# Filler products beside HGRN2's later levels and its last part, with a new order of the lanes and a reworked unit norm, in a one-core decoder layer

## The chip, the core and the metric

The kernel runs on one core of a Trainium2 chip. The metric is the device time of one execution in microseconds (us). The core has TensorE (PE, matrix products; PEld is its weight load), VectorE (DVE), ScalarE (ACT), GpSimd (POOL) and SyncE (SP, which issues transfers). Each engine works through its own queue in order, and the queues meet only at semaphores.

## The reference, cut to what matters

One decoder layer for 512 prompt tokens and 8 samples of 4 tokens (T = 544 columns in all): four mixers in parallel (block-sparse attention, Mamba-2, HGRN2, gated DeltaNet), an output projection, cross-attention to 256 memory tokens, and a SwiGLU network. All in float32. The parts that the change touches:

```python
def gla_chunked(q, k, v, log_f, s0):          # HGRN2
    ...
        att = jnp.einsum('blhk,bshk,blshk->blsh', qc, kc, dec)
        o = (jnp.einsum('blsh,bshv->blhv', att, vc)
             + jnp.einsum('blhk,bhkv->blhv', qc * jnp.exp(bcum), S))
    ...
def l2_norm(x, eps=1e-6):
    return x * lax.rsqrt(jnp.sum(x * x, axis=-1, keepdims=True) + eps)
    ...
    # gated DeltaNet, gdn_mixer
    q = l2_norm(q.reshape(b, L, GDN_HEADS, GDN_DK)) * GDN_DK ** -0.5
    k = l2_norm(k.reshape(b, L, GDN_HEADS, GDN_DK))
    beta = jax.nn.sigmoid(beta_raw)
    ...
        kb = kc * bc[..., None]               # beta times k; v is taken times beta too
```

The samples' block-sparse attention (`moba_sample`) reads 2048 past keys and values for each sample from a paged cache, 16 pages of 128 tokens each.

## The kernel before, in words

The work is a row of stages, and every engine passes `stage_ended` between them: inputs, `win` (input projection), `ssm` (Mamba-2 and HGRN2, with three other things beside them), `gdn`, `wout`, cross-attention, `wxo` with the first half of the network, `wdn`. The change lies in the stage `ssm`, which goes from about 283 to 554 us.

**The lanes.** In that stage each engine has four generators, and the string `LANES` (L2882) says in which order their steps are issued. All engines follow the same string, so it fixes the order of each engine's queue:

- `m` is the main lane: `ssm_tensor`/`ssm_vector`/`ssm_scalar` (19 steps), then `hgrn_tensor`/`hgrn_vector`/`hgrn_scalar` (22 steps). Of HGRN2, steps 20 to 27 are the eight prompt levels (j = 0 to 7: 16 products of 64x128 by 128 each, into banks 0 to 3), steps 28 to 30 the three sample levels, step 31 the first turn of the last part (`tail_tensor`), and steps 32 to 41 its five token tiles, two steps each, called here 0a, 0b, 1a, ... 4b. Step 18 is the last step of Mamba-2 with products.
- `p` is the samples' attention (`moba_sample_*`, 111 steps): 66 key steps k0 to k65 (turn four pages' worth of keys on TensorE, copy them on ScalarE, score the earlier ones), four steps without work for TensorE in which VectorE ranks the blocks (L1501 to L1517) and ScalarE takes the exponentials (L1553), five steps pt0 to pt4 that turn the probabilities, and 32 value steps v0 to v31, each one quarter of pages (four loads of 128 KB). There are NPG = 4 page buffers; the load of quarter n + 4 waits until quarter n has been used (`ms_values_used`), and SP and POOL issue the quarters in turn (`load_pages`, L449).
- `u` is the unit norm of DeltaNet's q and k (`unit_*`, 17 steps), and the spreading of beta over k and v. TensorE sums squares to 4 rows through `headsel`, ScalarE makes the inverse root on 4 partitions, and TensorE spreads the 4 rows over 128 partitions through `pairsel`: 8 products of 272 columns for the sums and 12 for the six spreads. VectorE multiplies out of PSUM banks 5 and 6.
- `n` is Mamba-2's norm (`ssm_norm_*`, 3 steps), through bank 4.

Before, seen from the `m` steps, the keys run until step 19; the norm is in the segments behind steps 20 to 22; pt0 is behind step 21; v0 and v1 are behind level 4 (step 24); the values then go two to a segment and end behind 3b; the unit norm goes from level 4 to 1b; the product `vpick` (L1443 on, out of the attention's result) stands ahead of 4b.

**A prompt level.** For level j + 1 VectorE writes differences (two operations), ScalarE takes their exponential (L2377), VectorE multiplies q and k by it, and then VectorE merges level j from PSUM (L2309, four operations). TensorE's next level waits for the products of q and k and for a free bank of the four.

**The last part** (`tail_tensor`, run = 0 for HGRN2). Step ia turns tile i + 1; step ib does the state and output products of tile i and waits for copies by VectorE (`tail_tok_out`).

`mm` (L257) is the plain product in float32 (recorded as two instructions each), `tr` (L260) the transpose, `bank(b)` one of eight PSUM banks of 512 columns. `ident` and `lev` are constants in SBUF.

Of the kernel before, what the change touches and what calls it, by code (L numbers as in the profile page):

```python
# [19 lines left out]
ALU = mybir.AluOpType  # L20
# [47 lines left out]
def build(nc, a, o):  # L68
# [7 lines left out]
    def S(name):  # L76
        if name not in sems:
            sems[name] = ctx.enter_context(nc.semaphore(name))
        return sems[name]

    with ctx:
# [25 lines left out]
        def bank(i):  # L107
            return PS[i // 2][:, i % 2, :]
# [5 lines left out]
        def carve(buf, at, *shape):  # L114
            n = 1
            for s in shape:
                n *= s
            v = buf[:, at:at + n]
            if len(shape) == 2:
                v = v.rearrange("p (a b) -> p a b", b=shape[1])  # L120
            elif len(shape) == 3:
                v = v.rearrange("p (a b c) -> p a b c", b=shape[1], c=shape[2])
            return v
# [133 lines left out]
        def mm(out, lhsT, rhs, start, stop):  # L257
            return nc.tensor.matmul(out, lhsT, rhs, start=start, stop=stop, skip_group_check=True)  # L258

        def tr(out, in_, k):  # L260
            return nc.tensor.transpose(out, in_, ident[0:k, 0:k])  # L261

# [117 lines left out]
        g_A = carve(PROJ, base + 2176, 2176)  # L380
        g_N = carve(PROJ, base + 2 * 2176, 2176)
        g_QK = carve(PROJ, base + 3 * 2176, 2176)
        g_sq = carve(XN, 2 * DH, 2, T)
        g_kb = carve(XN, 2 * DH, 2, T)
        g_norm = XN[0:H, 1216:1216 + T], SC[0:H, 8528:8528 + T]

        m = Carver(XN, 4 * T)
        t_tok = m(512)
# [995 lines left out]
        def moba_sample_tensor(pe):  # L1384
# [57 lines left out]
                yield  # L1442
            yield  # L1443
            pe.wait_ge(S("satt_o"), 1)
            pe.wait_ge(S("g_beta"), 6)
            pick = ident.rearrange("p (g e h t) -> p g e h t", e=2, h=H, t=TS)
            for e in range(2):
                for c_ in range(2):
# [202 lines left out]
        def half(ap, j):  # L1651
            return ap[:, j * HT:(j + 1) * HT]

        def spread_norm(pe, n):

            hp, kind = n % 2, n // 2
            src = rows[:, 2, :] if kind == 2 else g_norm[kind]
            for j in range(2):
                last = mm(bank(5 + j)[:, 0:HT], pairsel[0:H, hp, :], half(src, j), True, True)
            last.then_inc(S("rows_spread"), 1)  # L1660

        def unit_tensor(pe):
            yield
            for x in range(2):
                pe.wait_ge(S("satt_pt_out"), 5)
                pe.wait_ge(S("g_sq"), x + 1)
                if x:
                    pe.wait_ge(S("g_root"), 1)
                for hp in range(2):
                    for j in range(2):  # L1670
                        last = mm(bank(5 + j)[0:H, 0:HT], headsel[:, hp, :], half(g_sq[:, hp, :], j), hp == 0, hp == 1)
                last.then_inc(S("g_sum"), 1)
                yield
                yield
            pe.wait_ge(S("g_root"), 3)
            for n in range(6):
                if n:
                    pe.wait_ge(S("g_beta"), n)
                spread_norm(pe, n)
                yield  # L1680
                yield

        def unit_scalar(s):
            def squares(x):
                if x:
                    s.wait_ge(S("g_sum"), x)
                for hp in range(2):
                    last = A.activation(g_sq[:, hp, :], (gq, gk)[x][:, hp, :], ACT.Square)
                last.then_inc(S("g_sq"), 1)

            squares(0)
            yield
            yield
            for x in range(2):
                s.wait_ge(S("g_sum"), x + 1)
                for j in range(2):
                    last = A.activation(half(g_norm[x], j), two(5)[j][0:H, :], ACT.Ln, bias=eps[0:H, :])
                last.then_inc(S("g_root"), 1)
                if x == 0:
                    squares(1)  # L1700
                    yield
                    yield
            s.wait_ge(S("g_root"), 2)
            for x in range(2):
                last = A.activation(g_norm[x], g_norm[x], ACT.Exp, scale=-0.5)
            last.then_inc(S("g_root"), 1)
            yield
            for _ in range(12):
                yield

        def unit_vector(v):
            for _ in range(5):
                yield
            for n in range(6):
                yield
                hp, kind = n % 2, n // 2
                v.wait_ge(S("rows_spread"), 2 + n + 1)
                for j in range(2):
                    if kind == 0:
                        last = V.scalar_tensor_tensor(half(gq[:, hp, :], j), half(gq[:, hp, :], j), SCALE, two(5)[j], ALU.mult, ALU.mult)  # L1720
                    elif kind == 1:
                        last = tt(half(gk[:, hp, :], j), half(gk[:, hp, :], j), two(5)[j], ALU.mult)
                    else:
                        v.wait_ge(S("g_beta"), 4)
                        tt(half(g_kb[:, hp, :], j), half(gk[:, hp, :], j), two(5)[j], ALU.mult)
                        last = tt(half(gv[:, hp, :], j), half(gv[:, hp, :], j), two(5)[j], ALU.mult)
                last.then_inc(S("g_beta"), 1)
                yield


# [330 lines left out]
        def tail_tensor(pe, run, att, kd, qe, vT, kbg, N):  # L2061
# [17 lines left out]
            for i, (t0, w, _) in enumerate(TILES):  # L2079
# [22 lines left out]
                    last.then_inc(S("tail_w"), 1)  # L2102
                if i + 1 < NT:
                    turn(i + 1)
                yield
                pe.wait_ge(S("tail_tok_out"), 5 * run + i + 1)
                if gdn:
# [19 lines left out]
                if sample:  # L2127
                    pe.wait_ge(S("tail_vm"), run + 1)
                    for h in range(H):
                        r = slice((h % 2) * 64, (h % 2) * 64 + 64)  # L2130
                        last = mm(bank(tail_s_st[run][h // 2])[r, :], t_tok[0:w, h * 64:(h + 1) * 64], vm_of(run)[0:w, h * 512:(h + 1) * 512], True, True)
                    last.then_inc(S("tail_st"), 1)
                yield

        t_rt = sm(2, NS)
# [199 lines left out]
        def hgrn_tensor(pe):  # L2335
# [3 lines left out]
            for (lo, hi), nt, w, nl in lv_groups():  # L2339
                for j in range(nl):  # L2340
# [14 lines left out]
                        m_ += 1  # L2355
                    if j:
                        n += 1
                    yield
            yield from tail_tensor(pe, 0, h_att_of, h_k1[:, 0], h_q1[:, 0], proj[:, C_HI:C_HI + 2, :], None, None)

# [95 lines left out]
        def gdn_scalar(s):  # L2456
            hgrn_norm_scalar(s, 0)
            for i, (t0, w, _) in enumerate(TILES):
                s.wait_ge(S("g_m"), i + 1)
                ex = hl(g_p1[:, i % 4, :], w)  # L2460
                A.activation(ex, ex, ACT.Exp).then_inc(S("g_exp"), 1)
                if i < 4:
                    s.wait_ge(S("rows_spread"), 8 + i + 1)
                    A.activation(half(g_logd[:, i // 2, :], i % 2), bank(3 + 4 * (i % 2))[:, 0:HT], ACT.Copy).then_inc(S("rows_spread_out"), 1)
            s.wait_ge(S("rows_spread_out"), 4)
            link(A.activation(g_kbg, g_logd, ACT.Exp), "s")
# [408 lines left out]
        def mixer_lane(eng, ssm, hgrn):  # L2875
# [3 lines left out]
            yield from hgrn  # L2879


        LANES = "m".join(["pp"] + ["pppp", "ppp"] * 9 + ["ppp"] + ["ppn"] * 3 + ["pp"] + ["ppu"] * 7 + ["ppuu"] * 5  # L2882
                         + ["pp"] * 5 + ["p"])

        def lanes(main, pages_, unit, norm):
            steps = {"m": main, "p": pages_, "u": unit, "n": norm}
# [148 lines left out]
```

## Time and profile before

| | us |
|---|---|
| median of 3 runs | 1513.37 |
| lowest, highest | 1507.18, 1522.45 |
| the profiled execution, device time | 1517.02 |
| its span, first to last instruction | 1515.3 |
| TensorE busy in the span | 1358.2 (90%) |
| VectorE, ScalarE, GpSimd busy | 658.7, 467.9, 442.6 |
| mean granted TensorE clock | 0.907 of 2.4 GHz |

A granted clock of 1.00 is 2.4 GHz and 0.50 is 1.2 GHz; a value between them is a stretch in which both occur. Times of rows are us from the span's start. TensorE's matmul ends are modelled, so two neighbouring groups may overlap by some tenths of a microsecond.

### The profile page before, as it was taken

What the parts mean: (1) busy time and instruction counts of PE and PEld (TensorE: products, weight loads), DVE (VectorE), ACT (ScalarE), POOL (GpSimd) and SP (SyncE); (2) the same over time, 40 slices, a digit from 0 to 9 for tenths busy, and PEclk for the clock granted to TensorE, in tenths of its full rate; (3) what the DMA queues carried; (4) which work ended last, traced back from release to release, by engine and by line L of the source; (5) the groups of instructions that cost most, each with busy time, mean ns of one, the idle gap of its engine ahead of it and who ended that gap; (6) DMA issues with size and microseconds to landing.
All of it is one profiled execution on the core that took longest, in us unless ns stands there. A gap on an engine that the chain in (4) does not pass through costs nothing.

```text
span 1515.3 us, 24848 instructions
## 1 busy us (share of the span) xinstructions
PE 1358.2 (90%) x10080; PEld 1184.4 (78%) x10080; DVE 658.7 (43%) x1104; ACT 467.9 (31%) x769; POOL 442.6 (29%) x370
## 2 busy tenths in 40 slices
PE   5997999889767976888989898989899999989999
PEld 4997987656554556787879784439899999989998
DVE  4569944254665236653242924310763333330003
ACT  3322244254233014123345423203532222222221
POOL 5424431323103402003525050003234433434330
PEclk8998999879757556998969999999999999999999
DMA  4222230346306630003333040451223223222321
GB/s 122 79 62 70 74 114 1 118 147 192 106 0 196 183 111 1 1 7 119 112 113 98 29 167 22 169 185 56 70 76 93 84 86 96 84 77 77 91 64 60
DMA packets 177556, 136.85 MB, mean 90 GB/s; under 512 B 15011, under 2 KB 165972, under 8 KB 177442
## 3 DMA queue, kind: packets, MB, share of 16 engines
q1 hardware_dynamic: 167906, 113.85, 24.8%
q0 software_dynamic: 7200, 20.23, 4.4%
q8 instruction: 80, 1.31, 0.4%
q10 hardware_dynamic: 2336, 1.18, 0.3%
q14 instruction: 34, 0.28, 0.1%
HBM read 127.27 MB, written 7.96 MB: 89 GB/s over the span
## 4 chain that ended last, share of the span: by engine, by line
PE 75%; DVE 15%; ACT 4%; issue 2%; DMA 2%; POOL 1%; SPq 1%; DVEq 0%; POOLq 0%; ACTq 0%
PE PS L258 69%; PE PS L261 6%; DVE PROJ L1746 2%; DVE SC L626 1%; DVE PROJ L626 1%; DVE XN L887 1%; DVE XT L626 1%; DVE XN L626 1%; POOL W_LO L242 1%; DMA W_scratch<-in_cache_moba_v 1%; DVE PROJ L1747 1%; DVE XN_parts L878 1%; DVE RSQ L885 0%; DVE OM L1595 0%; DMA PROJ<-in_x_sample 0%
## 5 line engine op out<-in xcount | busy, mean ns | idle before, releaser
L242 POOL TENSOR_TENSOR W_LO<-W,W_HI 128x1024 fp32r<-128x1024 f32 (+1 forms) x130 | 317.3, 2445 | 797.8 <-ACT W_HI L233 797.8
L258 PE MATMUL PS<-XN_parts,W_HI 128*128 128x272 f32 x1184 | 341.9, 289 | 0.0
L258 PE MATMUL PS<-OM_parts,W_HI 128*128 128x272 f32 x960 | 279.0, 291 | 0.0
L258 PE MATMUL PS<-SC_parts,W_HI 128*128 128x272 f32 (+2 forms) x832 | 246.7, 296 | 14.7 <-POOL W_LO L242 13.5
L258 PE MATMUL PS<-SC_parts,W_LO 128*128 128x272 f32 (+2 forms) x832 | 243.1, 292 | 0.0
L258 PEld LDWEIGHTS PS<-XN_parts,W_HI 128*128 128x128 f32 x1184 | 224.6, 190 | 0.0
L258 PE MATMUL PS<-OM_parts,W_LO 128*128 128x272 f32 x704 | 203.9, 290 | 0.0
L233 ACT ACTIVATE W_HI<-W 128x1024 fp32r<-128x1024 f32 (+1 forms) x130 | 134.1, 1041 | 207.5 <-PE PS L258 207.5
L258 PEld LDWEIGHTS PS<-OM_parts,W_HI 128*128 128x128 f32 x960 | 183.2, 191 | 0.1
L258 PEld LDWEIGHTS PS<-SC_parts,W_HI 128*128 128x128 f32 x832 | 159.3, 191 | 19.3 <-POOL W_LO L242 12.5
L258 PEld LDWEIGHTS PS<-SC_parts,W_LO 128*128 128x128 f32 x832 | 159.1, 191 | 0.0
L258 PE MATMUL PS<-PROJ_parts,W_HI 128*128 128x272 f32 (+2 forms) x608 | 153.1, 294 | 5.0 <-DVEq L2873 5.0
L258 PEld LDWEIGHTS PS<-OM_parts,W_LO 128*128 128x128 f32 x704 | 132.3, 188 | 0.0
L258 PEld LDWEIGHTS PS<-PROJ_parts,W_HI 128*128 128x128 f32 x608 | 109.1, 193 | 5.4 <-DVEq L2873 5.3
L258 PE MATMUL PS<-PROJ_parts,W_LO 128*128 128x272 f32 (+2 forms) x256 | 75.7, 296 | 0.0
L258 PE MATMUL PS<-SC,XN 64*64 64x4 f32 (+3 forms) x384 | 69.6, 327 | 0.0
L449 POOL DMA_DIRECT2D W_scratch<-in_cache_moba_v x64 | 34.3, 536 | 113.8 <-PE PS L258 83.4
L626 DVE TENSOR_TENSOR SC<-SC 128x272 f32<-128x272 f32 (+6 forms) x68 | 36.8, 544 | 70.5 <-ACT SC L820 50.9
L1147 ACT ACTIVATE PROJ<-PS 128x512 f32<-128x512 f32 (+1 forms) x76 | 44.9, 597 | 65.1 <-PE PS L261 52.8
L261 PE MATMUL PS<-CN,W_scratch 128*128 128x128 f32 x272 | 51.4, 319 | 14.1 <-ACT SC L1554 12.2
L258 PE MATMUL PS<-SC 64*128 64x128 f32 (+7 forms) x404 | 52.7, 345 | 11.7 <-DVE PROJ L626 5.2
L258 PE MATMUL PS<-PROJ,XN 128*128 128x128 f32 (+3 forms) x280 | 43.3, 306 | 20.1 <-DVE XN L626 19.6
(375 smaller groups left out, 2259.6 us busy)
## 6 DMA issues: line engine op xcount, KB each, us to landing
W<-in_w_gu SPq DMA_DIRECT2D x44, 512.0 KB, 3.7
W<-in_w_in SPq DMA_DIRECT2D x30, 512.0 KB, 3.6
W_scratch<-in_cache_moba_k SPq DMA_DIRECT2D x64, 128.0 KB, 2.7
W_scratch<-in_cache_moba_k POOLq DMA_DIRECT2D x64, 128.0 KB, 2.6
W_scratch<-in_cache_moba_v SPq DMA_DIRECT2D x64, 128.0 KB, 2.1
W_scratch<-in_cache_moba_v POOLq DMA_DIRECT2D x64, 128.0 KB, 2.8
W<-in_w_xkv SPq DMA_DIRECT2D x16, 512.0 KB, 3.5
W<-in_w_down SPq DMA_DIRECT2D x16, 512.0 KB, 3.6
```

The costliest lines, as they stand in the source:

```text
L233: nc.scalar.activation(hi_lo(n)[0], raw_chunk(n), ACT.Copy)\
L242: nc.gpsimd.tensor_tensor(hi_lo(n)[1], raw_chunk(n), hi_lo(n)[0].bitcast(F32), ALU.subtract).then_inc(S("weights_split"), 1)
L258: return nc.tensor.matmul(out, lhsT, rhs, start=start, stop=stop, skip_group_check=True)
L261: return nc.tensor.transpose(out, in_, ident[0:k, 0:k])
L449: eng.dma_start(pages[:, n % NPG, i, :], cache[0].rearrange("g p h d -> g p (h d)")[bass.ds(ids[i], 1)].rearrange("g p n -> (g p) n"))\
L626: return V.tensor_tensor(out, x, y, op)
L878: V.scalar_tensor_tensor(lo(k)[:, TOKENS[run][j]], XT[:, k, TOKENS[run][j]], par(GAINS[run][1] + k), hi(k)[:, TOKENS[run][j]].bitcast(F32) ...
L887: last = V.scalar_tensor_tensor(xn[:, k, c_], xn[:, k, c_], par(GAINS[run][0] + k), rsq[:, c_], ALU.mult, ALU.mult)
L1147: return A.activation(o_, i_, ACT.Copy)
L1746: V.scalar_tensor_tensor(dst[:, d:SEQ], src[:, 0:SEQ - d], wt[3 - d], dst[:, d:SEQ], ALU.mult, ALU.add)
L1747: last = V.scalar_tensor_tensor(ds_, win_[:, :, 3 - d:7 - d], wt[3 - d], ds_, ALU.mult, ALU.add)
```

## The change

1. `warm(b, n)` is new: n products of the constant `ident` (128x128) with 512 columns of the constant `lev`, into bank b, which nobody reads. It is called in `hgrn_tensor` behind the products of prompt level 4 (8 products) and of levels 5, 6 and 7 (2 each), into bank 4; and in `tail_tensor` for run 0 in steps 0a to 3a and 0b to 2b (2 each), into bank 2. That makes 28 products.
2. `LANES` is rewritten. Now the key steps go four to a segment and end behind step 17; the step with the blocks' ranking and the exponentials is still behind level 1; the norm is behind steps 20 to 22; pt0 and pt1 are behind level 3, pt2 and pt3 behind level 4, pt4 and v0 behind level 5, then values two to a segment; v29, v30 and v31 are behind 4a, and `vpick` behind 4b. The unit norm's nine steps start behind the last sample level and end behind 3a.
3. The unit norm works on full rows: ScalarE squares one 128x544 tile (`g_sqs`, three buffers), TensorE sums it with the block matrix `blk64` (two products of 272 columns, result on all 128 partitions), ScalarE takes Ln and Exp, VectorE multiplies once from SBUF. Four such units, then two spreads of beta as before: 12 products in place of 20.

```diff
@@ build @@
+        def warm(b, n):
+            for _ in range(n):
+                mm(bank(b), ident, lev[:, 0:4, :].rearrange("p a b -> p (a b)"), True, True)
...
-        g_sq = carve(XN, 2 * DH, 2, T)
+        g_sqs = [carve(XN, 2 * DH + i * T, T) for i in range(3)]
...
@@ moba_sample_tensor @@
             pe.wait_ge(S("satt_o"), 1)
-            pe.wait_ge(S("g_beta"), 6)
+            pe.wait_ge(S("g_beta"), UNITS + 2)
@@ unit_tensor @@
+        UNITS = 4
+        UNIT_STEPS = 9
...
         def unit_tensor(pe):
+            for x in range(UNIT_STEPS):
+                n = x - 1
+                if 0 <= n < UNITS:
+                    if n == 0:
+                        pe.wait_ge(S("satt_pt_out"), 5)
+                    else:
+                        pe.wait_ge(S("g_root"), 2 * n - 1)
+                    pe.wait_ge(S("g_sq"), n + 1)
                     for j in range(2):
+                        last = mm(bank(5 + j)[:, 0:HT], blk64, half(g_sqs[n % 3], j), True, True)
+                    last.then_inc(S("g_sum"), 1)
+                elif x in (5, 7):
+                    if x == 5:
+                        pe.wait_ge(S("g_root"), 2 * UNITS - 1)
+                    else:
+                        pe.wait_ge(S("g_beta"), UNITS + 1)
+                    for j in range(2):
+                        last = mm(bank(5 + j)[:, 0:HT], pairsel[0:H, x // 7, :], half(rows[:, 2, :], j), True, True)
+                    last.then_inc(S("rows_spread"), 1)
                 yield
+        def unit_scalar(s):
+            for x in range(UNIT_STEPS):
+                n = x - 2
+                if 0 <= n < UNITS:
+                    s.wait_ge(S("g_sum"), n + 1)
+                    for j in range(2):
+                        last = A.activation(half(g_sqs[n % 3], j), two(5)[j], ACT.Ln, bias=eps)
+                    last.then_inc(S("g_root"), 1)
+                    s.wait_ge(S("g_root"), 2 * n + 1)
+                    A.activation(g_sqs[n % 3], g_sqs[n % 3], ACT.Exp, scale=-0.5).then_inc(S("g_root"), 1)
+                if x < UNITS:
+                    if x == 3:
+                        s.wait_ge(S("g_beta"), 1)
+                    A.activation(g_sqs[x % 3], unit_of(x), ACT.Square).then_inc(S("g_sq"), 1)
                 yield
         def unit_vector(v):
+            for x in range(UNIT_STEPS):
+                n = x - 2
+                if 0 <= n < UNITS:
+                    v.wait_ge(S("g_root"), 2 * n + 2)
+                    V.scalar_tensor_tensor(unit_of(n), unit_of(n), SCALE if n < 2 else 1.0, g_sqs[n % 3], ALU.mult, ALU.mult)\
+                        .then_inc(S("g_beta"), 1)
+                elif x in (6, 8):
...
@@ tail_tensor @@
                 if i + 1 < NT:
                     turn(i + 1)
+                if run == 0 and i < 4:
+                    warm(2, 2)
                 yield
...
                     last.then_inc(S("tail_st"), 1)
+                if run == 0 and i < 3:
+                    warm(2, 2)
                 yield
@@ hgrn_tensor @@
                     if j:
                         n += 1
+                    if w == P and j >= 4:
+                        warm(4, 8 if j == 4 else 2)
                     yield
@@ lanes @@
-        LANES = "m".join(["pp"] + ["pppp", "ppp"] * 9 + ["ppp"] + ["ppn"] * 3 + ["pp"] + ["ppu"] * 7 + ["ppuu"] * 5
-                         + ["pp"] * 5 + ["p"])
+        LANES = "m".join(["pp"] + ["pppp"] * 14 + ["ppp"] * 3 + ["p", "p", "pn", "pn", "n", "pp", "pp", "pp"] + ["pp"] * 4
+                         + ["ppu"] * 9 + ["pp", "pppp", "pp"])
```

## Rows read from the trace of the kernel before

**Rows 1.** Page, part 2: busy tenths and TensorE's granted clock, 40 slices.
```profile
PE   5997999889767976888989898989899999989999
...
PEclk8998999879757556998969999999999999999999
```
**Rows 2.** Page, part 4: the chain that ended last, by engine.
```profile
PE 75%; DVE 15%; ACT 4%; issue 2%; DMA 2%; POOL 1%; SPq 1%; DVEq 0%; POOLq 0%; ACTq 0%
```
**Rows 3.** Windows, TensorE: stretch, length, busy (instructions), granted clock, DMA share, GB/s.
```profile
444.00:455.00 11.00, 8.88 (x52) 0.50 0.01 1
460.00:473.00 13.00, 12.94 (x152) 1.00 0.53 172
473.00:477.00 4.00, 0.51 (x16) 0.91 0.73 240
489.00:506.00 17.00, 16.85 (x92) 0.50 0.60 180
506.00:523.00 17.00, 17.00 (x95) 0.50 0.51 148
523.00:532.00 9.00, 8.68 (x75) 0.94 0.71 201
538.00:551.00 13.00, 12.85 (x94) 0.50 0.00 0
551.00:585.00 34.00, 25.76 (x136) 0.50 0.29 93
```
**Rows 4.** Timeline, TensorE, 392 to 447 us: start, length; idle before in brackets.
```profile
392.36 3.69 PE L258 MATMUL PS<-PROJ,SC 32*128 32x512 f32 x8
395.99 0.43 PE L258 MATMUL PS<-PROJ,W 128*32 128x128 f32 x8
...
399.57 0.43 PE L258 MATMUL PS<-PROJ,W 128*32 128x128 f32 x8 [0.33 <-ACT PROJ L1147]
...
409.44 5.10 PE L258 MATMUL PS<-SC 64*128 64x128 f32 x32 [5.15 <-DVE PROJ L626]
426.69 1.12 PE L261 MATMUL PS<-CN,W_scratch 128*128 128x128 f32 x4 [12.15 <-ACT SC L1554]
427.60 2.02 PE L258 MATMUL PS<-SC,CN 128*128 128x272 f32 x4
429.55 5.13 PE L258 MATMUL PS<-SC 64*128 64x128 f32 x32
...
446.12 5.10 PE L258 MATMUL PS<-SC 64*128 64x128 f32 x32 [3.22 <-DVE PROJ L2309]
```
**Rows 5.** Timeline, VectorE, 411 to 440 us.
```profile
411.00 0.74 DVE L1501 SCALAR_TENSOR_TENSOR W_scratch<-XN,SM,W_scratch 128x512 f32<-128x512 f32 x1
...
436.42 3.53 DVE L1972 RECIPROCAL RSQ<-RSQ 128x544 f32<-128x544 f32 x1
```
**Rows 6.** Timeline, ScalarE, 431 to 433 us.
```profile
431.55 1.06 ACT L2377 ACTIVATE W<-W 128x1024 f32<-128x1024 f32 x1
```
**Rows 7.** Timeline, TensorE, 453 to 537 us.
```profile
453.15 1.94 PE L258 MATMUL PS<-W_scratch,PROJ 128*32 128x256 f32 x16
...
471.80 0.32 PE L258 MATMUL PS<-PROJ,W 64*32 64x32 f32 x8
...
477.12 1.93 PE L258 MATMUL PS<-W_scratch,PROJ 128*32 128x256 f32 x16 [3.61 <-DMA W_scratch<-in_cache_moba_v]
...
489.15 0.69 PE L261 MATMUL PS<-CN,SC 128*128 128x128 f32 x2 [5.66 <-DVE SC L626]
...
492.06 2.18 PE L258 MATMUL PS<-XN,CN 4*128 4x272 f32 x4
...
509.66 0.70 PE L258 MATMUL PS<-XN 128*64 128x64 f32 x8
...
515.02 1.93 PE L258 MATMUL PS<-W_scratch,PROJ 128*32 128x256 f32 x16
...
535.16 1.08 PE L258 MATMUL PS<-W_scratch,PROJ 128*32 128x256 f32 x8 [1.15 <-DMA W_scratch<-in_cache_moba_v]
```

More of the change, by code:

```diff
@@ L382, in build @@
         g_QK = carve(PROJ, base + 3 * 2176, 2176)
-        g_sq = carve(XN, 2 * DH, 2, T)
+        g_sqs = [carve(XN, 2 * DH + i * T, T) for i in range(3)]
         g_kb = carve(XN, 2 * DH, 2, T)
-        g_norm = XN[0:H, 1216:1216 + T], SC[0:H, 8528:8528 + T]
         m = Carver(XN, 4 * T)
@@ L1652, in half @@
             return ap[:, j * HT:(j + 1) * HT]
[L1654 to L1660, printed above, removed]
-        def unit_tensor(pe):
[L1663 to L1669, printed above, removed]
-                    for j in range(2):
[L1671 to L1680, printed above, removed]
+        UNITS = 4
@@ new lines, in build, with unit_of @@
+        UNIT_STEPS = 9
+        def unit_of(n):
+            return (gq, gk)[n // 2][:, n % 2, :]
+        def unit_tensor(pe):
+            for x in range(UNIT_STEPS):
[6 more added lines that the diff above has]
+                    pe.wait_ge(S("g_sq"), n + 1)
+                    for j in range(2):
+                        last = mm(bank(5 + j)[:, 0:HT], blk64, half(g_sqs[n % 3], j), True, True)
[8 more added lines that the diff above has]
+                    last.then_inc(S("rows_spread"), 1)
@@ L1681, in unit_tensor @@
                 yield
         def unit_scalar(s):
[L1684 to L1708, printed above, removed]
+            for x in range(UNIT_STEPS):
[11 more added lines that the diff above has]
+                    A.activation(g_sqs[x % 3], unit_of(x), ACT.Square).then_inc(S("g_sq"), 1)
@@ L1709, in unit_scalar @@
                 yield
         def unit_vector(v):
[L1712 to L1724, printed above, removed]
+            for x in range(UNIT_STEPS):
[5 more added lines that the diff above has]
+                elif x in (6, 8):
+                    hp = x // 8
+                    v.wait_ge(S("rows_spread"), 2 + hp + 1)
+                    v.wait_ge(S("g_beta"), UNITS)
+                    for j in range(2):
@@ L1725, in unit_vector @@
                         tt(half(g_kb[:, hp, :], j), half(gk[:, hp, :], j), two(5)[j], ALU.mult)
                         last = tt(half(gv[:, hp, :], j), half(gv[:, hp, :], j), two(5)[j], ALU.mult)
-                last.then_inc(S("g_beta"), 1)
+                    last.then_inc(S("g_beta"), 1)
                 yield
@@ L2462, in gdn_scalar @@
                 if i < 4:
-                    s.wait_ge(S("rows_spread"), 8 + i + 1)
+                    s.wait_ge(S("rows_spread"), 4 + i + 1)
                     A.activation(half(g_logd[:, i // 2, :], i % 2), bank(3 + 4 * (i % 2))[:, 0:HT], ACT.Copy).then_inc(S("rows_spread_out"), 1)
```

## The prediction, made before the changed kernel was run

> **What bounds the kernel now.** I began with the page's busy slices. TensorE is at 8 or 9 tenths for most of the span, but of slices 10 to 15 (379 to 606 us) five are at 6 or 7, and it is there that the granted clock falls to 5 to 7 tenths [rows 1]. The chain that ended last is 75% TensorE and 15% VectorE [rows 2]. So a microsecond of TensorE work taken from that stretch counts, and one added counts too, unless TensorE stands waiting there anyway. The windows then give the clock by stretch [rows 3]: 0.50 at 444 to 455 (early levels), 1.00 at 460 to 473 (levels 6 and 7), falling after the idle stretch 473 to 477, then 0.50 through 489 to 523 although TensorE is busy in 33.85 of those 34 us, 0.94 at 523 to 532, and 0.50 again for the samples' tile (538 to 551) and the first part of the next stage (551 to 585). The timeline shows what ends each wait: VectorE (5.15 us ahead of level 1, 3.22 ahead of level 4, 5.66 ahead of the last part's first turn), the softmax's exponentials (12.15 us ahead of pt0), and transfers of value pages (3.61 us, 1.15 us) [rows 4, 7]. The stretch is therefore three things by turns: a chain through VectorE and ScalarE up to level 4, TensorE at one clock or the other in the later levels and the last part, and transfers where a quarter's buffer came free late.
>
> A change of this kernel has to be over about 1%, 15 us, to be told from none.
>
> **Prices.** Four products of 512 columns took 3.69 us at full clock, 0.92 each [rows 4]; two of 272 columns took 2.02 us at half clock [rows 4], and half of that at full is taken as 1.0. By columns one filler product at half clock is 1.85 to 1.9 us. The filler loads 128 weight rows where the 3.69 us row loads 32; bounds 0.85 and 1.0 us at full clock, and I take 0.92. The 28 products cost 26 us at full clock and 52 at half.
>
> **Keys four to a segment.** Before, k61 to k65 come after Mamba-2's last products (the 3.69 us row at 392.36) and fill 395.99 to 400.0, while VectorE already runs the chain that ends in level 1 at 409.44 [rows 4]. In the new string these five steps stand ahead of those products. TensorE's sum is the same, but the chain starts 4.0 us later with nothing beside it. L1501 (0.74 us, behind level 0's merge before [rows 5]) now stands ahead of level 1's differences. Level 1 is thus 4.7 us late, at 414.1. Bounds: 0, if waits in the key steps hide it, to 6.
>
> **Levels 2 and 3 ahead of pt0.** The 12.15 us wait for the exponentials goes from TensorE's queue: level 2 (5.13 us) now runs in it [rows 4]. But level 3 needs the exponential at 431.55 [rows 6], which on ScalarE stands behind the softmax's. That comes 4 us later with everything, and about 1.9 earlier because pt0's copy (0.6) and the wait for it (1.2) no longer stand in front: 433.6. Level 3 then starts at about 436.7, where it stood before; but VectorE's reciprocal of 3.53 us, at 436.42 before [rows 5], starts at about 438.7, and the differences of level 4 come after it. Level 4 starts 2.2 us later: 446.1 becomes 448.3 [rows 4]. What leaves TensorE's wait is late next on VectorE. Bounds -3 and +6.
>
> **Level 4 to the sample levels.** Before, v0 is used at 453.15 and the first sample level is at 471.80 [rows 7]. After: level 4 5.1 us at half clock, to 453.4; eight fillers. Before the clock rose some 13 us after level 4 began; with dense products I let it rise some 9 us after, so two fillers at 1.85 and six at 0.92 make 9.2, and with a third nearer half 9.7: to 463.1. Then pt2 and pt3 1.2, level 5 2.8 (half the 5.1), two fillers 1.85, pt4 and the own block 1.6: v0 at 470.5, 17 us later than before. Then v0, level 6, fillers, two values, level 7, fillers, two values: 0.5 + 2.8 + 1.85 + 1.1 + 2.8 + 1.85 + 1.1 = 12.0, plus 0.7 of small waits: first sample level at 483.2, 11.4 late. Two fillers a level hide in part behind VectorE (some 6 us a level), the eight do not. Bounds: 7.4 us for the eight if the clock rises at once, 14.8 if not before they end.
>
> **Sample levels to the first turn.** Before 471.8 to 489.15, 17.35 us: values with the 3.61 us wait [rows 7], two spreads, then VectorE's and ScalarE's preparation. From 477.12 on, two values, a spread and the level (1.9 + 2.2 + 0.4) end at 481.6, and the turn comes 7.5 later, 0.7 of it a norm product of VectorE that moves away. After: v3 and v4 are used at about 482.5; a quarter's reload took about 7 us where two were used together (v6 and v7 just ahead of 471.8, v10 at 477.1, less the time before the issue), so v7 and v8 are there at 490, the last sample level at 491.2, the turn 6.8 later: 498, 8.9 late. The waits for pages replace the spreads.
>
> **The last part.** Before: 489.15 to 536.2 (the end of v31) = 47.0 us [rows 7]. After, at half clock: a first half-step is two turns 1.3, two fillers 3.7, two values 1.94, a unit sum 2.0, together 8.9; at full 4.7. A second half-step with state is 5.4 at half (509.66 to 515.02 [rows 7]) and 3.0 at full, with fillers, values and sum 7.0 at full. TensorE stands still from about 492 to 498, so it starts at half clock; I let it be full from the middle of 0a: turn segment 5.3, 0a 7.5, 0b 4.4, 1a 4.7, 1b 7.0, 2a 3.7, 2b 7.0, 3a 3.7, 3b 4.1 = 47.4, to 545.4. The 14 fillers here (13 to 15 us) use up what full clock and the smaller unit norm give. Then v29, v30, v31 stand together behind 4a; v31's buffer is freed by v27, used at about 544.5, and its load takes about 7 us (v27's release to v31 took some 8 before, which is the 1.15 us wait at 535.16 [rows 7]): v31 ends at 552.5, 16.3 late.
>
> The unit norm loses 8 of 20 products. The nearest price for a spread is 2.18 us at half clock [rows 7]; 8 products are 8.7 us at half, 4 at full, and this is inside the sums above. On ScalarE a unit is two table loads, two halves of Ln, an Exp and a Square, which I estimate at under 5 us, in a stretch where ScalarE has no other work; VectorE loses operations. I cost it at nothing beyond that; if VectorE waits for an exponential, up to 1 us a unit.
>
> **The end.** Before, `vpick` and the wait ahead of it (2.4 us) came between v31 and the samples' tile; now they follow. 16.3 - 2.4 = +13.9. Nothing behind the stage is edited, and TensorE has another idle stretch there, so its clock at 551 to 585 is left at 0.50.
>
> **Sum.** 4.7, then 2.2, 11.4, 8.9, 16.3 and 13.9 are the lateness at each point, not terms to be added; the stage ends 13.9 us later: 1517.0 + 13.9 = 1531 against the profiled execution. That one is 3.7 us over the median of 1513.4, so the forecast in the terms of the median is 1527 us, 0.9% more. Its own range by the bounds above is 1514 to 1540.
>
> A rule against the trace. TensorE was busy in 33.85 of 34 us at 489 to 523 and its clock stayed at 0.50 [rows 3]. The Trainium skill (TensorE: Matmul & The Clock Gate, section Why this matters for your kernels) says to keep TensorE busy without gaps and it reaches the full clock. By that rule the last part would need no fillers, only unbroken work; this trace does not agree.
>
> **Rivals.**
> *The clock stays up (not slower).* The fillers raise the clock in the first of the eight (-2.3), it outlives the 6 us wait ahead of the last part (-5), the samples' tile runs at full clock (12 us become 7, -5), and so does the start of the next stage, where 25.8 busy us at half [rows 3] would fall by about 8 with VectorE's chain next in line. 13.9 - 20.3 = -6.4: 1510.6 against the profiled execution, 1507 in the median's terms. It decides itself at the idle stretch ahead of the turn: if the granted clock is still 1.00 in the first turn, this one holds. For it: the clock did hold from 523 to 532 with like work. Against: it fell after 473 to 477. [...]
> *The order of the lanes costs less than counted (same).* The key steps' waits hide the 4.7 us, and the page reloads keep ahead: the values lose only the fillers' time, about +3: 1520, or 1516 in the median's terms. For it: TensorE waits at few of the key steps, and SP and POOL are idle beside. Against: the wait of 3.61 us on a transfer.
> *The fillers don't lift the clock in the last part (slower).* Then 14 fillers cost 26 us, and the segments sum to 5.3 + 8.9 + 9.4 + 8.9 + 13.1 + 6.9 + 13.1 + 6.9 + 7.3 = 79.8 in place of 47.4; with v31 no longer waiting, some 28 us more: 1559, or 1555. For it: the busy stretch at 0.50. Against: the fillers use all rows and columns, where the work before had 4, 32 or 64.
>
> **How the numbers follow.** Forecast 0.42, clock stays up 0.25, order cheap 0.20, no lift 0.13. Faster by over 1%: 0.16 of the second and 0.04 of the third, 0.20. Slower by over 1%: 0.19 of the first (it stands just under the bound), 0.02 of the third, 0.13: 0.34. Within 1%: 0.46. The range reaches from 1500 (the clock stays up, with a little more from the smaller norm) to 1552; that leaves out the worse half of the last rival and the best end of the second.
>
> **What would show it.** Right: in the changed kernel's timeline level 1 starts at about 414, level 4 at 448, v0 at 470 or later, the first turn at 498, TensorE's clock 1.00 from about 510 to 545, and a wait on a value transfer ahead of v31. Wrong: v0 before 462; the clock at 1.00 in the samples' tile or at 555; or half clock between 510 and 540.

## The result, and the profile after

The changed kernel takes 1523.5 us (median of 20 runs, 1515.06 to 1531.08), the one before 1514.01 us (20 runs, 1507.18 to 1522.45). The ratio is 1.0059 with a 95% interval of 1.0043 to 1.0076: 9 us slower. The forecast was 1527. The profiled execution of the changed kernel took 1521.28 us with a span of 1519.7, that is 2.2 under its median, and the one of before was 3.0 over its own, so the spans of the two profiles lie only 4.4 us apart (1519.7 and 1515.3) where the medians lie 9.5 apart.

TensorE's timeline of the changed kernel, with the lines that answer to [rows 4, 7] (start, length, form, idle before it):

```profile
391.73 7.19 PE L258 MATMUL PS<-PROJ,SC 32*128 32x512 f32 x8
...
413.08 4.60 PE L258 MATMUL PS<-SC 64*128 64x128 f32 x32 [4.21 <-DVE PROJ L631]
...
421.03 5.10 PE L258 MATMUL PS<-SC 64*128 64x128 f32 x32 [2.24 <-DVE PROJ L2305]
435.90 5.10 PE L258 MATMUL PS<-SC 64*128 64x128 f32 x32 [9.76 <-DVE PROJ L2305]
...
447.16 4.62 PE L258 MATMUL PS<-SC 64*128 64x128 f32 x32 [5.13 <-DVE PROJ L2305]
451.71 7.13 PE L258 MATMUL PS<-CN 128*128 128x512 f32 x16
...
465.90 0.64 PE L258 MATMUL PS<-W_scratch,PROJ 128*32 128x256 f32 x8
...
477.80 0.32 PE L258 MATMUL PS<-PROJ,W 64*32 64x32 f32 x8
...
483.51 1.93 PE L258 MATMUL PS<-W_scratch,PROJ 128*32 128x256 f32 x16 [4.14 <-DMA W_scratch<-in_cache_moba_v]
...
488.01 1.94 PE L258 MATMUL PS<-W_scratch,PROJ 128*32 128x256 f32 x16 [2.20 <-DMA W_scratch<-in_cache_moba_v]
492.80 0.69 PE L266 MATMUL PS<-CN,SC 128*128 128x128 f32 x2 [2.86 <-DVE SC L631]
...
542.17 2.79 PE L258 MATMUL PS<-W_scratch,PROJ 128*32 128x256 f32 x24 [5.34 <-DMA W_scratch<-in_cache_moba_v]
...
561.71 3.97 PE L258 MATMUL PS<-SC,CN 128*128 128x272 f32 x8 [3.61 <-DVE SC L631]
```

In order: Mamba-2's last products (now at half clock, 7.19 us), levels 1, 2, 3 and 4, the eight fillers (7.13 us, all at full clock), v0, the first sample level, two waits for value pages, the first turn of the last part, v29 to v31, and the first products of the next stage. (The helper's transposes are L266 here, L261 before.)

The windows that answer to [rows 3] (stretch, length, busy, granted clock, DMA share, GB/s):

```profile
451.00:459.00 8.00, 8.00 (x27) 0.99 0.00 0
459.00:477.00 18.00, 17.64 (x148) 1.00 0.27 82
477.00:493.00 16.00, 6.80 (x89) 0.65 0.66 210
493.00:498.50 5.50, 5.50 (x28) 0.50 0.78 238
498.50:536.50 38.00, 38.00 (x278) 0.99 0.64 198
545.00:557.00 12.00, 12.00 (x80) 0.50 0.00 1
562.00:587.00 25.00, 24.89 (x129) 0.50 0.36 123
```

With the fillers in place the clock is 1.00 in the later levels and 0.99 over 38 us of the last part, where before it was 0.50 at 489 to 523; whether it is the fillers that raise it, run a1 below decides. The samples' tile and the next stage's start stay at 0.50. And the last part did not end earlier: from the turn (492.80) to the end of v31 (544.96) are 52.2 us, 47.0 before, with 5.34 us of waiting for pages ahead of v29. Counted from level 1, the turn comes at the same place in both kernels (79.7 us), v31 ends 5.1 us later, and the next stage follows v31 2.4 us sooner, since `vpick` has moved.

### The profile page after: what moved, and what is told of

Its sections match the earlier page's. It is cut to its first block, busy times and chain, and to the rows that moved or that the text cites. A ratio compares the mean times of both kernels' runs of the same rounds, so it can differ in the third digit from the quotient of the medians.

```text
span 1519.7 us, 24935 instructions
## 1 busy us (share of the span) xinstructions
PE 1358.7 (89%) x10120; PEld 1180.8 (78%) x10120; DVE 658.5 (43%) x1100; ACT 476.3 (31%) x779; POOL 442.7 (29%) x370
## 4 chain that ended last, share of the span: by engine, by line
PE 55%; DVE 7%; ACT 2%; issue 2%; POOL 1%; DMA 1%; POOLq 0%; DVEq 0%; ACTq 0%
PE PS L258 53%; PE PS L266 2%; DVE PROJ L631 1%; DVE XT L631 1%; DVE XN L892 1%; DVE SC L631 1%; DVE XN L631 1%; DVE XN_parts L883 1%; DVE RSQ L890 0%; POOL W_LO L242 0%; DMA W_scratch<-in_cache_moba_v 0%; POOL PROJ_parts L242 0%; POOLq L444 0%; DVE OM L2687 0%; ACT W_HI L233 0%
## 5 line engine op out<-in xcount | busy, mean ns | idle before, releaser
L258 PE MATMUL PS<-SC 64*128 64x128 f32 (+7 forms) x404 | 50.4, 331 | 24.7 <-DVE PROJ L2305 17.1
L258 PEld LDWEIGHTS PS<-SC 64*128 64x128 f32 (+5 forms) x404 | 41.2, 215 | 34.0 <-DVE SC L631 23.1
L258 PE MATMUL PS<-SC,XN 64*64 64x4 f32 (+3 forms) x384 | 66.4, 318 | 0.0
L258 PE MATMUL PS<-OM_parts,PROJ_parts 128*128 128x272 f32 x256 | 55.2, 307 | 2.9 <-DVE XN_parts L883 1.6
```

## The experiments

The stretch up to Mamba-2's last products starts some microseconds earlier or later from execution to execution (389 to 398 us over these runs), so traces are compared from level 1 of HGRN2 to the first products of the next stage. This table has both readings for every run; the ratios are to the kernel before, timed beside it (its median was 1514.01 to 1515.93 us in the four rounds). Medians are of 20 executions for the first two rows, of 6 for d1, and of 9 to 12 for the others.

| run | level 1 to next stage, us | median, us | ratio (95%) |
|---|---|---|---|
| before | 146.0 | 1514.01 | |
| changed | 148.6 | 1523.50 | 1.0059 (1.0043 to 1.0076) |
| a1, no fillers | 139.3 | 1517.66 | 1.0016 (0.9994 to 1.0038) |
| a2, fillers in the levels only | 145.9 | 1520.21 | 1.0035 (1.0017 to 1.0054) |
| a3, fillers in the last part only | 142.4 | 1517.34 | 1.0021 (0.9994 to 1.0048) |
| a4, before plus fillers | 151.2 | 1522.72 | 1.0051 (1.0028 to 1.0073) |
| b1, before plus new unit norm | 145.2 | 1518.73 | 1.0023 (1.0005 to 1.0042) |
| b3, changed, values earlier | 149.5 | 1521.54 | 1.0039 (1.0014 to 1.0064) |
| c1, no fillers, keys as before | 139.1 | 1513.40 | 0.9994 (0.9972 to 1.0015) |
| c2, c1 with the reciprocal late | 132.7 | 1508.82 | 0.9964 (0.9942 to 0.9985) |
| d1, c2 with pt0, pt1 earlier | 130.4 | 1502.41 | 0.9922 (0.9892 to 0.9952) |
| d2, c2 with fillers in a wait | 134.4 | 1508.91 | 0.9962 (0.9940 to 0.9983) |
| d3, a1 with half value loads | 138.4 | 1515.58 | 0.9999 (0.9978 to 1.0019) |
| d4, changed with half value loads | 146.3 | 1524.16 | 1.0056 (1.0035 to 1.0077) |

The two columns do not say the same everywhere. The stretch is read from one execution of each kernel. That of c1 is 6.9 us shorter than before and its median is the same; that of c2 is 13.3 us shorter and its median some 5.5 us. What stands behind the stretch took between 955.9 and 964.3 us in these traces, where no edit touches it. The runs do not show where the difference goes, so a claim about the whole time rests on the ratio, and the stretch tells only where in the stage time was won or lost.

**a1 to a4: the fillers by themselves.** The theory after the result: the fillers buy the full clock in the last part and are worth about what they cost. The rival: they only cost.

```diff
 a1, a2:            (tail_tensor)
-                if run == 0 and i < 4:
-                    warm(2, 2)
...
-                if run == 0 and i < 3:
-                    warm(2, 2)
 a1, a3:            (hgrn_tensor)
-                    if w == P and j >= 4:
-                        warm(4, 8 if j == 4 else 2)
```

a4 puts the same lines into the kernel before. Expected:

> The changed kernel without its 28 filler products; new lanes and new unit norm stay. Theory (the fillers buy the full clock in the last part and are worth about what they cost): the last part runs at half clock for most of its length, v31 ends at 544 to 549 us (changed kernel: 544.9), and the time is within 4 us of the changed kernel's 1523.5. Rival (the fillers only cost): 26 us of products at full clock fall away and nothing slows, 1498.

> Only the 14 fillers behind levels 4 to 7. Theory: the turn ahead of the last part stays at 492 to 493, the last part runs at 0.50 for most of its length and takes 50 us or more in place of 43.5, time 1526 to 1531. Rival (the clock raised in the levels carries through, or needs no fillers): the last part takes 43.5 - 13 = 30 us or is held by page loads at 40, 1512 to 1518.

> Only the 14 fillers of the last part. Theory: v0 comes 5 to 7 us earlier than 465.9, the turn at 488 to 490, the last part at full clock as in the changed kernel, time 1518 to 1521. Rival (the eight fillers are free because VectorE or the page loads set the pace there): turn at 492 to 493 and 1522 to 1525.

> The kernel before with the 28 fillers at the same places; its own lanes and unit norm. Theory: the later levels lose some 6 us, the last part runs at full clock but with 14 fillers and takes as long as before (47 us), v31 at 541 to 543, time 1519 to 1521. Rival (the whole loss of the change is in the lanes, fillers neutral or better): 1508 to 1514.

Without fillers the changed kernel is 5.8 us faster (1523.50 against 1517.66), and its stretch 9.3 us shorter. Neither theory holds as it stood: not a draw, and not 26 us either. The two halves add up: from a1, the level fillers alone add 6.6 us to the stretch (a2) and those of the last part 3.1 (a3), together 9.7 against 9.3 measured. By the medians a2 adds 2.6 and a3 nothing, which is less than the 5.8 of both together; the intervals are too wide to say more. In a2 the turn stayed where it was counted from level 1 (80.3 us, 79.7 in the changed kernel), as expected, but the last part took 48.8 us and neither time forecast held. In a3 v0 came 7.2 us earlier counted from level 1 and the median lies just under the 1518 to 1521 expected. In the order of before (a4) the fillers cost 5.2 us of the stretch, ratio 1.0051, near the 1519 to 1521 expected. There they did shorten the last part, from 47.1 to 42.9 us, but the way from level 1 to it grew by 7.4 us and what follows v31 by 2.0.

The premise itself fell. This is TensorE of a1, with no filler anywhere:

```profile
471.06 0.32 PE L258 MATMUL PS<-PROJ,W 64*32 64x32 f32 x8
...
486.83 0.69 PE L266 MATMUL PS<-CN,SC 128*128 128x128 f32 x2 [2.76 <-DVE SC L631]
...
496.32 1.45 PE L258 MATMUL PS<-W_scratch,PROJ 128*32 128x256 f32 x16 [1.89 <-DMA W_scratch<-in_cache_moba_v]
...
521.34 1.93 PE L258 MATMUL PS<-W_scratch,PROJ 128*32 128x256 f32 x16 [3.70 <-DMA W_scratch<-in_cache_moba_v]
...
532.37 1.94 PE L258 MATMUL PS<-W_scratch,PROJ 128*32 128x256 f32 x16 [4.53 <-DMA W_scratch<-in_cache_moba_v]
535.89 1.08 PE L258 MATMUL PS<-W_scratch,PROJ 128*32 128x256 f32 x8 [1.59 <-DMA W_scratch<-in_cache_moba_v]
...
553.73 3.96 PE L258 MATMUL PS<-SC,CN 128*128 128x272 f32 x8 [3.61 <-DVE SC L631]
```

and its windows (stretch, length, busy, granted clock, DMA share, GB/s):

```profile
491.00:497.00 6.00, 4.11 (x53) 0.99 0.81 245
497.00:500.00 3.00, 3.00 (x14) 0.50 0.69 220
500.00:515.00 15.00, 12.86 (x116) 0.99 0.78 242
515.00:532.00 17.00, 9.14 (x80) 0.77 0.66 191
```

The last part starts at 486.83 and the clock is at 0.99 in 491 to 497 and 500 to 515 without any filler. What it meets then are pages: six waits in the last part, 13.9 us in all (2.8 before). v31 ends at about 537, 50 us after the turn; TensorE was busy for little more than half of 515 to 532. In a2 the clock was 1.00 at 510 to 525, again without fillers in that part. So most of the full clock was to be had without fillers once the order and the unit norm were new, and it was worth little, because a faster TensorE runs into the page loads. What the fillers cost is less than their own time because part of them stands where TensorE would have waited: from 456 to 546 us it waits 11.7 us for value pages in the changed kernel and 20.0 in a1.

**b1: is it the unit norm that lifts the clock?** The kernel before with the new `unit_*` functions only:

```diff
-        LANES = ... + ["ppu"] * 7 + ["ppuu"] * 5 + ["pp"] * 5 + ["p"]
+        LANES = ... + ["ppu"] * 9 + ["pp"] * 8 + ["p"]
```

> The kernel before with the new unit norm only: its own lanes, the nine unit steps one to a segment from level 4 to the last part's first turn, no fillers. Theory (the unit sums through the block matrix fill all rows and columns, and that, not the fillers, is what holds the clock up in the last part): granted clock over 0.85 from 495 to 525 where it was 0.50, stage end 5 to 8 us earlier counted from level 1, time 1508 to 1511. Rival (it only saves eight products): the last part stays at 0.50, time 1511 to 1515.

In between: the granted clock is 0.75 at 495 to 510 and 0.70 at 510 to 525 (0.50 and 0.53 before), the stretch only 0.8 us shorter, and the ratio 1.0023. The time forecast missed: I had 1508 to 1511. TensorE's waits for pages after the turn grew from 2.8 to 9.7 us here as well, and two waits on ScalarE's squares' chain (2.27 and 1.84 us) came in before it, since here the unit steps stand beside the levels, where ScalarE and VectorE are busy. The last part itself took 42.3 us in place of 47.1, but its first turn came 2.7 us later counted from level 1. That the sums over all rows and columns are what raises the clock is thus likely, not shown: b1 changes ScalarE's and VectorE's part with the sums and has gaps that the kernel before does not have, and no run changes the sums alone.

**b3: the three values behind 4a.**

```diff
-         + ["ppu"] * 9 + ["pp", "pppp", "pp"]
+         + ["ppu"] * 3 + ["pppu", "ppu", "pppu"] + ["ppu"] * 3 + ["pp", "pp", "pp"]
```

> The changed kernel with two value steps moved forward: three behind 0b and 1b, one behind 4a (before three behind 4a). Theory (v31's load waits for v27 alone): the 5.3 us wait ahead of v29 falls to about 1, time 3 to 4 us under the changed kernel, 1519 to 1521. Rival (the transfers are at their rate and the wait only moves): sum of page waits in the last part unchanged, 1522 to 1525.

Neither held in full. From 456 to 546 us TensorE waited 10.8 us for pages in six places, in the changed kernel 11.7 us in three; from the first turn on it is 4.1 us in three places against 5.3 in one:

```profile
486.19 1.94 PE L258 MATMUL PS<-W_scratch,PROJ 128*32 128x256 f32 x16 [4.65 <-DMA W_scratch<-in_cache_moba_v]
```

This wait of b3, its longest, stands ahead of the turn and answers to the 4.14 us at 483.51 in the changed kernel. The last part took 49.9 us (52.2), but the turn came 3.1 us later counted from level 1, and that was lost ahead of the edit for the most part: v0 was already 2.5 us later, in a place where the two kernels are the same. 1521.54 against 1523.50 is inside the uncertainty, so whether moving the values is worth 2 us isn't shown.

**c1 and c2: the order of the keys, and VectorE's reciprocal.**

```diff
 c1 (on a1): key segments as before, segment 20 "ppn"
 c2 (on c1): third step of the norm lane
-  ... "ppn", "pn", "n", ... "ppu", "pp", "pppp", "pp"
+  ... "ppn", "pn", "",  ... "ppu", "ppn", "pppp", "pp"
```

> The changed kernel without fillers, and with the key steps in the order of the kernel before (four and three in turn, Mamba-2's last products ahead of k61). Theory (the keys' packing delays the chain to level 1 by 4.7 us): level 1 starts 13.5 us after the end of Mamba-2's last products again but with five key steps beside it, and the time is 3 to 6 us under the run without fillers, 1511 to 1514. Rival (the packing costs nothing): equal to the run without fillers, 1516 to 1518.

> As the one before, and the norm's last step on VectorE (reciprocal and two products, 5 us) moves from behind level 2 to behind 3b. Theory (VectorE's chain sets levels 3 to 4): level 4 starts 5 us earlier counted from level 1 (29 in place of 34), the stage ends 3 to 5 us earlier, time 1506 to 1511. Rival (the values' page loads take it all back): level 4 earlier, but v31 within 1 us, time unchanged.

c1 is 4.3 us under a1, as expected, and the stretch behind level 1 is the same (139.1 and 139.3): what the keys' packing costs comes before level 1. The intervals of c1 and a1 overlap, so the size is uncertain. From the start of Mamba-2's last products to level 1 are 17.7 us in c1, 17.1 before, and 21.4 in a1 and in the changed kernel, where those products run at half clock (7.19 us in place of 3.69). In b3, with the same order of keys, they happened to run near full clock (3.93 us) and the distance was 18.1; so most of the longer distance is the clock. The forecast's reason, that five key steps of 4.0 us stand ahead of these products and no longer beside VectorE's chain, can't be read from the traces, because the start of these products moves by more than that from one execution to another; both costs together would be over 4.3 us. c2 shows VectorE's chain: level 4 starts 30.5 us behind level 1 (34.9 in c1, 34.1 in the changed kernel, 36.7 before), the stretch is 6.4 us shorter than c1's, and the kernel is faster than the one before, 0.9964. The time came as the theory said, and the stretch gained more than its 3 to 5 us. The theory's rival, in which the page loads take it all back, did not come:

```profile
409.33 5.10 PE L258 MATMUL PS<-SC 64*128 64x128 f32 x32 [5.15 <-DVE PROJ L631]
...
432.94 5.10 PE L258 MATMUL PS<-SC 64*128 64x128 f32 x32 [9.76 <-DVE PROJ L2301]
...
439.87 5.13 PE L258 MATMUL PS<-SC 64*128 64x128 f32 x32
...
476.50 0.69 PE L266 MATMUL PS<-CN,SC 128*128 128x128 f32 x2 [2.65 <-DVE SC L631]
```

**d1 and d2: what else stands in that wait.** TensorE still waits 9.76 us ahead of level 3 there (432.94 above is its start). d1 puts pt0 and pt1 into it; d2 puts fillers into it.

```diff
 d1 (on c2)
-  ... "ppn", "pn", "", ... "ppn", "pppp", "pp"
+  ... "ppn", "pn", "pp", ... "ppn", "pp", "pp"
 d2 (on c2, hgrn_tensor, behind level 2)
+                    if w == P and j == 2:
+                        warm(6, 5)
```

> As the run with the late reciprocal, and pt0, pt1 stand behind level 2 (in TensorE's 9.8 us wait), everything after them two steps earlier, so that 4a has v31 alone. Theory (the last part is paced by the reload of page buffers, so its end follows v0): v0 4 to 6 us earlier counted from level 1, v31 and the stage's end 4 to 7 us earlier, time 1502 to 1506. Rival (TensorE sets the pace): end moves by under 2 us, 1507 to 1510.

> As the run with the late reciprocal, and five fillers (bank 6) behind level 2, in the 9.8 us in which TensorE waits for VectorE. Theory (fillers cost nothing in a wait and raise the clock for levels 3 to 5): level 3 starts within 0.5 us of before, levels 3 and 4 take 2.8 us in place of 5.1, v0 3 to 5 us earlier, time 1505 to 1508. Rival (the clock stays at 0.50 and five fillers of 1.85 us end late, or VectorE sets levels 3 to 5): v0 unchanged within 1 us, 1508 to 1511.

TensorE of d1 (level 1, pt0 with pt1, the samples' own block ahead of v0, the turn, v31, the samples' tile, the next stage):

```profile
408.74 5.10 PE L258 MATMUL PS<-SC 64*128 64x128 f32 x32 [5.15 <-DVE PROJ L631]
...
426.00 1.97 PE L266 MATMUL PS<-CN,W_scratch 128*128 128x128 f32 x8 [3.42 <-ACT SC L1559]
...
443.57 1.13 PE L258 MATMUL PS<-W 32*128 32x256 f32 x4 [0.36 <-ACT W L1152]
...
475.92 0.69 PE L266 MATMUL PS<-CN,SC 128*128 128x128 f32 x2 [3.14 <-DVE SC L631]
...
519.19 0.64 PE L258 MATMUL PS<-W_scratch,PROJ 128*32 128x256 f32 x8 [1.76 <-DMA W_scratch<-in_cache_moba_v]
522.65 0.30 PE L258 MATMUL PS<-PROJ,XN 32*64 32x32 f32 x2 [2.82 <-DVE XN L2154]
...
539.12 3.97 PE L258 MATMUL PS<-SC,CN 128*128 128x272 f32 x8 [3.61 <-DVE SC L631]
```

The own block, and v0 behind it, come 34.8 us after level 1 in place of 41.8 in c2 (451.14 - 409.33), and the stage ends 2.3 us earlier. The median is 1502.41, ratio 0.9922 (0.9892 to 0.9952): this version beats both kernels, 11.6 us under the one before and 21 under the changed one (six executions), and has no filler. v0 moved by 7.0 us, the first turn by nothing (67.2 us behind level 1 in both; its wait is ended by VectorE), the end of v31 by 4.9 and the stage's end by 2.3. So the earlier values did not bring the turn forward, v31 came as early as the theory said, and half of that was lost again in 2.82 us of waiting for VectorE ahead of the samples' tile, which c2 does not have. The theory's 4 to 7 us at the stage's end did not come, though the time did (6.4 us by the medians, more than the trace of one execution explains).

d2 is the fair test of a filler that costs nothing:

```profile
423.44 5.39 PE L258 MATMUL PS<-CN 128*128 128x512 f32 x10
433.27 5.10 PE L258 MATMUL PS<-SC 64*128 64x128 f32 x32 [4.44 <-DVE PROJ L2301]
```

The five products took 5.39 us, at full clock for most of it, and level 3 started as late as in c2 (23.6 us behind level 1 both times). But 4.44 us of idle followed, and level 3 ran its 5.10 us at half clock all the same. v0 came 1.7 us earlier than in c2 and the next stage 1.7 later, and the time equals c2's (1508.91 and 1508.82), inside the rival's range. The theory was right that the fillers fit into the wait, and wrong about what follows. Here a raised clock that wasn't followed by work at once was lost.

**d3 and d4: bytes or issue?** Each value quarter is loaded by half its columns, so half of the sample attention's values is left out of both kernels.

```diff
+                w_ = 2 * P if n < 32 else P
-                    eng.dma_start(pages[:, n % NPG, i, :],
+                    eng.dma_start(pages[:, n % NPG, i, 0:w_],
```

> The changed kernel without fillers, and the value pages loaded by half their columns (the other half of each buffer keeps what was there; half of the attention's values is left out). Theory (page transfers set the pace of the last part once its clock is high): waits on value transfers in the last part fall from 13.9 us to under 4, the stage ends 7 to 10 us earlier, time 1507 to 1511. Rival (the waits are latency, not bytes): 1515 to 1519.

> The changed kernel with all its fillers and the same half loads (the same half of the values left out). Theory: the 4.1 and 2.2 us waits ahead of the last sample levels and the 5.3 us ahead of v29 shrink, time 1514 to 1518, and the fillers now cost more against the run without them (8 to 12 us, 6.5 with full loads), because less of them stands in page waits. Rival (fillers earn their clock): the two runs with half loads within 3 us.

Of d3 the rival won. With half the bytes the stretch shortens by 0.9 us (d3 against a1) and 2.3 (d4 against the changed kernel), and the times stay: 1515.58 and 1517.66, 1524.16 and 1523.50. From 456 to 546 us TensorE waited 19.7 us for value pages in d3 and 20.0 in a1. In d4 these waits fell from 11.7 to 9.9 us only, and its time forecast, 1514 to 1518, failed; that the fillers would cost 8 to 12 us with half loads came right (8.6 by the medians). GpSimd's timeline tells why. d3, then a1:

```profile
486.49 2.29 POOL L455 DMA_DIRECT2D W_scratch<-in_cache_moba_v  x4 [2.26 <-issue]
491.04 2.29 POOL L455 DMA_DIRECT2D W_scratch<-in_cache_moba_v  x4 [2.26 <-issue]
...
500.46 2.29 POOL L455 DMA_DIRECT2D W_scratch<-in_cache_moba_v  x4 [2.27 <-issue]
```

```profile
504.69 2.29 POOL L454 DMA_DIRECT2D W_scratch<-in_cache_moba_v  x4 [2.26 <-issue]
509.25 2.29 POOL L454 DMA_DIRECT2D W_scratch<-in_cache_moba_v  x4 [2.26 <-issue]
514.01 0.55 POOL L454 DMA_DIRECT2D W_scratch<-in_cache_moba_v  x1 [2.47 <-issue]
517.31 1.72 POOL L454 DMA_DIRECT2D W_scratch<-in_cache_moba_v  x3 [2.75 <-issue]
...
526.13 2.29 POOL L454 DMA_DIRECT2D W_scratch<-in_cache_moba_v  x4 [2.26 <-issue]
```

A quarter is four transfers of 2.29 us together, behind 2.26 us without a recorded operation; in the chain of waits these hold the reads of the four page numbers (L444, 0.29 us each recorded) and the gaps between them. That makes one quarter every 4.55 us from this queue, with 64 KB transfers as with 128 KB ones. GpSimd issues every second quarter, so two value steps cannot take less than 4.55 us for long, whatever TensorE's clock. In a1 the queue runs so without a rest from 472 to 533 us, all quarters from v7 to v31. The one exception is v25's, whose four transfers took 5.02 us because of a pause of 2.75 us behind the first (514.01 and 517.31 above); every trace of this case has it, its cause isn't shown, and behind it stands a1's 3.70 us wait. No run gave GpSimd fewer quarters to issue, so the issue rate is read from the timelines and not tested by an edit; what the edits rule out is the bytes.

In the changed kernel three quarters between 500 and 520 us wait for TensorE to free their buffer (their issues start at 501.87, 506.72 and 518.14, each 0.68 us behind the last use of the buffer). Behind them it is the queue that holds. The same queue ahead of v31:

```profile
531.06 1.70 POOL L454 DMA_DIRECT2D W_scratch<-in_cache_moba_v  x3 [0.33 <-issue]
535.02 2.29 POOL L454 DMA_DIRECT2D W_scratch<-in_cache_moba_v  x4 [2.26 <-issue]
539.57 2.29 POOL L454 DMA_DIRECT2D W_scratch<-in_cache_moba_v  x4 [2.25 <-issue]
```

The starts 535.02 and 539.57 are again 4.55 apart; they are v29's quarter and v31's. v31's buffer was free at 536.40, when v27 had been used, but the queue came to it 3.2 us later, 2.5 us more than those 0.68; it landed at 543.68, just ahead of its use at 543.85. The 5.34 us wait itself is for v29. Its buffer was free at 532.28, its issue began 2.7 us later, and its last transfer landed at 542.04, 5.3 us after that transfer was issued, where the median from 500 to 546 us is 2.7. SP issued a load of 512 KB in between, at 535.62; whether that is what delayed v29 isn't shown.

## Why the prediction was right, point by point

- **Direction and time.** Forecast 1527, 0.9% more; measured 1523.5, 0.6% more. That the path to the end of v31 gets longer was right, and its size was too large. That the fillers are partly paid back by the clock was not: a1 has most of that clock without them, and what made them cheap is that some stand in page waits. The last part's 54.5 us, forecast from a clock that the fillers buy, is therefore near the measured 52.2 in part by luck.
- **Keys four to a segment.** Forecast level 1 4.7 us late (414.1). It starts at 413.08, 3.6 late in one trace, and by c1 against a1 the packing costs 4.3 us. The size is right, the reason only in part at best: Mamba-2's last products fell to half clock, which was not foreseen, and that alone is 3.5 us.
- **Levels 2 and 3 ahead of pt0.** Forecast level 4 at 448.3; it is at 447.16. Right, and its reason too: VectorE's reciprocal stood in the chain, and c2, which moves it away, starts level 4 3.6 us earlier behind level 1 than the changed kernel.
- **Level 4 to the sample levels.** Forecast 11.4 us late (483.2), measured 6.0 (477.80). The term that was too large is the eight fillers: 9.7 forecast, 7.13 measured, for the clock had risen within level 4 (4.62 us in place of 5.10). That is 3.1 of the 5.4 us; another 1.1 is the earlier start of level 4. v0 came at 465.90, not 470.5.
- **To the first turn.** Forecast 8.9 us late, measured 3.65. The waits for pages came (4.14 and 2.20 us) as forecast.
- **The last part.** Forecast 54.5 us from the turn to the end of v31, measured 52.2; the clock was full from 498.5, near the middle of 0a as assumed. The wait ahead of v29 came (5.34 us). Its cause was named only in part: I had a reload of about 7 us that starts when v27 has been used. From v27's use to v31's landing were 7.3 us, as forecast, but 2.5 of them are GpSimd's queue, which issues a quarter every 4.55 us, and the wait that TensorE had was for v29, ahead of it. Halving the transfers (d3, d4) does not help.
- **The price of not having the fillers.** "The 14 fillers here use up what full clock and the smaller unit norm give" was wrong in its first half: most of the last part had the full clock without them (a1, a2). The rival in which the clock stays at 0.50 in spite of the fillers did not come either.
- **The clock stays up** (samples' tile, next stage): did not happen, 0.50 in both, and 0.50 in the first turn (493.00 to 498.50). **The order costs less than counted**: in part; without the fillers the order and the norm are at 1.0016 (0.9994 to 1.0038), and the key steps' cost was there.
- **The end.** Forecast 13.9 us later at the next stage's start, 6.3 in this pair of traces, of which 3.6 lie ahead of level 1. By the medians it is 9.5 us, so the two traces explain two thirds of it.

## What to carry to other kernels

Before products are added to hold a clock, ask what a TensorE at full clock would wait for next: here GpSimd's queue issues a page quarter every 4.55 us, and in a1 TensorE at full clock only changed half-speed work into waits. In these runs a filler did not pay where a gap followed it (d2) or where the clock was high without it (a1); the 14 beside the last levels and the 14 of the last part together cost about 6 us. The gain lay in the order: a 5 us VectorE step taken out of the chain, and steps put into a wait of TensorE, made the kernel 0.8% faster with no filler at all, with the new unit norm kept (alone, in b1, it gained nothing).

## What the runs showed that I had not expected

- Issuing, not bytes: with 64 KB in place of 128 KB a transfer, GpSimd's quarter still took 4.55 us, and the page waits stayed at 19.7 us (20.0).
- TensorE at 0.50 for 34 busy us in the kernel before [rows 3], and at 0.99 in the same part of a1, which does the same work in another order and with a smaller unit norm, and has gaps of 1 to 2 us in it (491 to 515, apart from 3 us at 0.50). Being busy without gaps was not enough. The Trainium skill (TensorE: Matmul & The Clock Gate, section Why this matters for your kernels) asks for unbroken work to reach the full clock; the trace of the kernel before does not agree with it.
- A clock raised by 5.39 us of fillers was gone after 4.44 us of idle (d2).
- A product of 128 rows by 512 columns cost 0.89 us at full clock (7.13 us for eight), no more than one with 32 rows (0.92).
